# Router logits taken from unscaled residual rows, with the norm's gain folded into the router weights

## The chip, the cores and the metric

The kernel runs on one core of one Trainium2 chip. The metric is the device time of one execution in microseconds. TensorE (PE) multiplies and transposes, VectorE (DVE), ScalarE (ACT) and GpSimd (POOL) work on vectors, SyncE (SP) issues most of the transfers and POOL issues the indexed ones.

## What is computed

One inference step of two layers over 576 rows (512 prompt rows and 64 sample rows) of width 1024. Layer 0 mixes rows with a banded attention, layer 1 with a convolution module. Each mixer is followed by a mixture of experts: 4 groups of 8 experts, the best group, and in it the best two experts.

```python
xt  = rms_norm(x, norm_ffn)                     # x * rstd(row) * gain(column)
g   = softmax(xt @ w_group + b_group);          g_w, g_idx = top_k(g, 1)
e   = xt @ w_router + b_router                  # 32 logits, 8 of each group
v, i = top_k(e[group g_idx], 2);                w2 = softmax(v)
y   = sum over the two experts: g_w * w2 * (silu(xt @ w_gate) * (xt @ w_up)) @ w_down
x   = x + y
```

## The kernel before

All matrices are float32. The 576 rows are five tiles, numbers 0 to 4; tile 4, the last, has 64 rows. Each engine runs a fixed list of instructions and waits on counting semaphores; `steps.done` makes an engine wait for its own instruction. The order around the change is written out by hand.

**The projection stage** ends each mixer. TensorE runs `project_pe`: for each tile j two halves of 512 columns, eight matmuls each (L421); the last tile's halves are interleaved in `both_halves` (L435). Between them stand the router's small jobs for the tiles ahead: `turn_pe` transposes a tile (8 transposes, L346), `logits_pe` multiplies it with the 36 router columns (L954), `ranks_pe` (L966, L967) counts rows per expert, and `table_pe` (L977) builds a table of the rows that each expert takes.

**VectorE** runs `project_dve`: `add(j, h)` adds a projected half to the residual `x` and counts `proj_ev` (L466); in layer 1 a full-width bias is added first (L475). `norm_dve` takes the reciprocal of the row's root (L327, from ScalarE's square sum and root, L320 and L321) and writes `x * ss * gain` to `xf` (L332), counting `normed`. `turn_dve` copies the second half of the transposed tile out of PSUM (L358), ScalarE's `turn_act` the first. `choose_dve` picks group and experts in three parts (L997 to L1001, L1005 to L1010, L1012 to L1024), `slots_dve` (L1029 to L1036) and `table_dve` (L1046 to L1051) work out where the rows go. The last `table_dve` ends the stage and counts `tabled`.

**SyncE** runs `first_loads(l, 1)` through this stage, strictly in order. For tiles 0 to 3 it waits for `normed` and stores the tile of `xf` to `x_rows` in HBM (L1371). Then:

```python
sp.wait_ge(proj_mm, 2 * TILES * (l + 1))
gu_load(sp, l, 1, (0,))            # 2 MB
x_store(TILES - 1)                 # waits for normed of the last tile
gu_load(sp, l, 1, (1,))            # 2 MB
gu_load(sp, l, 2, (0,))            # 2 MB
gu_part(sp, l, 2, 1, ONE, 0, UNSHARED)   # 0.5 MB
```

In layer 1 one more load of 2 MB (`dn_load`, L1357) stands behind these.

**The experts.** GpSimd waits for `x_out` (all five stores landed) and `tabled`, and fetches the rows of the first two expert pairs from `x_rows` with indexed transfers (`rows_in`, L1112). TensorE bridges the time with `keep_running` (L1188; 12 matmuls, which stand in the trace as 24), transposes the rows of pair 0 (L1195), and runs 16 pairs: up and gate (L1205) and down (L1224). The weights of a later pair are issued as TensorE frees their place; for pair 3 this happens in three parts during the first pair's L1205.

Of the kernel before, what the change touches and what calls it, by code (L numbers as in the profile page):

```python
# [7 lines left out]
ALU = mybir.AluOpType  # L8
# [3 lines left out]
P = 128  # L12
# [32 lines left out]
def encoder(nc, x_prompt, x_sample, cache_attn_k, cache_attn_v, cache_conv,  # L45
# [10 lines left out]
    C = D // P  # L56
# [29 lines left out]
    with ExitStack() as ctx:  # L86
        def sb(name, shape, dt=F32):
            return ctx.enter_context(nc.sbuf_tensor(name, shape, dt))

        def sem(name):  # L90
            return ctx.enter_context(nc.semaphore(name))
# [22 lines left out]
        mean_w = sb("mean_w", [P, P])  # L114
        router_w = sb("router_w", [P, C, RC])
        router_b = sb("router_b", [P, RC])
        logits = sb("logits", [P, TILES, RC])
        ss = sb("ss", [P, 3, TILES])
        eps = sb("eps", [P, 1])
# [55 lines left out]


        xf = xt_flat[:].rearrange("p (j d) -> p j d", j=TILES)
        xf_pc = xt_flat[:].rearrange("p (j q c) -> p j c q", j=TILES, c=C)
        xw = work[:, 0:C * TOKENS].rearrange("p (c t) -> p c t", c=C)
        junk = work[:, C * TOKENS:C * TOKENS + D]  # L180
        EARLY_TILES = 4 * C * FE // D - TILES
# [91 lines left out]
        op_mm = sem("op_mm"); op_ev = sem("op_ev"); krow_mm = sem("krow_mm"); krow_ev = sem("krow_ev")  # L273
        kv_out = [sem(f"kv_out{s}") for s in range(2)]

        first_up = sem("first_up"); proj_mm = sem("proj_mm"); proj_ev = sem("proj_ev")

        route_mm = sem("route_mm"); gates_max = sem("gates_max"); gates_exp = sem("gates_exp"); picks = sem("picks"); ranks = sem("ranks"); summed = sem("summed")
        routed = sem("routed"); ranked = sem("ranked"); placed = sem("placed"); far_routed = sem("far_routed")
# [56 lines left out]

        def turn_pe(pe, n, j):
            r, at = rows[j], TILES * n + j
            pe.wait_ge(normed, at + 1)
            if at >= 2:  # L340
                pe.wait_ge(turn_ev_a, at - 1)
                pe.wait_ge(turn_ev_d, at - 1)
            src = xf_pc if n % 2 else xn_pc
            for c in range(C):
                b = bank[TURN_BANKS[at % 2][c // 4]]
                mm = nc.tensor.transpose(b[:, (c % 4) * P:(c % 4) * P + r], src[0:r, j, c, :],  # L346
                                         ident[0:r, 0:r])
            mm.then_inc(turned, 1)
# [17 lines left out]
        def norms_act(act, steps, n):  # L366


            for j in range(TILES + 1):
                if j >= 1 and n % 2:  # L370
                    turn_act(act, n, j - 1)
                if j < TILES:
                    norm_act(act, steps, n, j)
                if j >= 1 and n % 2 == 0 and n < 2 * LAYERS:
                    turn_act(act, n, j - 1)
# [82 lines left out]

        def project_dve(dve, steps, l, bias_row):
            LAST = TILES - 1  # L460

            def add(j, h):
                dve.wait_ge(proj_mm, 2 * TILES * l + 2 * j + h + 1)
                r, cols = rows[j], slice(h * HALF, (h + 1) * HALF)
                src = bank[3][h * DEC:(h + 1) * DEC, :] if j == LAST else bank[h if l == j == 0 else 3 + h][0:r, :]
                nc.vector.tensor_tensor(x[0:r, j, cols], x[0:r, j, cols], src, ALU.add).then_inc(proj_ev, 1)  # L466

            for j in range(TILES):
                if j == LAST:
                    turn_dve(dve, 2 * l + 1, j - 1)  # L470
                    table_dve(dve, steps, l, j - 3)
                    slots_dve(dve, steps, l, j - 2)
                if bias_row is not None:
                    r = rows[j]
                    steps.done(nc.vector.tensor_tensor(x[0:r, j, :], x[0:r, j, :], bias_row[0:r, :], ALU.add))  # L475
                add(j, 0)
                if j == LAST:
                    add(j, 1)
                    choose_dve(dve, steps, l, j - 1, 0)
                    norm_dve(dve, steps, 2 * l + 1, j)  # L480
                    choose_dve(dve, steps, l, j - 1, 1)
                    turn_dve(dve, 2 * l + 1, j)
                    choose_dve(dve, steps, l, j - 1, 2)
                    continue
                if j >= 1:
                    turn_dve(dve, 2 * l + 1, j - 1)
                    if j >= 3:
                        table_dve(dve, steps, l, j - 3)
                    for part in range(3):
                        choose_dve(dve, steps, l, j - 1, part)  # L490
                add(j, 1)
                norm_dve(dve, steps, 2 * l + 1, j)
                if j >= 2:
                    slots_dve(dve, steps, l, j - 2)
            choose_dve(dve, steps, l, LAST, 0)
            table_dve(dve, steps, l, LAST - 2)
            slots_dve(dve, steps, l, LAST - 1)
            choose_dve(dve, steps, l, LAST, 1)
            choose_dve(dve, steps, l, LAST, 2)
            table_dve(dve, steps, l, LAST - 1)  # L500
            slots_dve(dve, steps, l, LAST)
            table_dve(dve, steps, l, LAST)
# [432 lines left out]


        def logits_at(j):
            return bank[4 if j >= TILES - 2 else 5][0:rows[j], 0:RC]

        def logits_pe(pe, l, j):  # L940
            pe.wait_ge(turn_ev_a, TILES * (2 * l + 1) + j + 1)
            pe.wait_ge(turn_ev_d, TILES * (2 * l + 1) + j + 1)
            if j == 0:
                pe.wait_ge(small_in, 64 * (l + 1))
            if j == TILES - 1:
                pe.wait_ge(picks, TILES * l + j - 1)
            elif j == TILES - 2:
                pe.wait_ge(proj_ev, 2 * TILES * l + 2 * (j + 1))
            elif TILES * l + j >= 1:
                pe.wait_ge(picks, TILES * l + j)  # L950
                if j >= 2:
                    pe.wait_ge(tabled, TILES * l + j - 1)
            for c in range(C):
                mm = nc.tensor.matmul(logits_at(j), xw[:, c, j * P:j * P + rows[j]], router_w[:, c, :],  # L954
                                      start=c == 0, stop=c == C - 1)
            mm.then_inc(route_mm, 1)
# [31 lines left out]
        def choose_dve(dve, steps, l, j, part):  # L988
# [5 lines left out]
            few = down_iota[0:r, EXPERTS - GROUPS:EXPERTS]  # L994
            if part == 0:
                dve.wait_ge(route_mm, TILES * l + j + 1)
                do(V.tensor_tensor(logits[0:r, j, :], logits_at(j), router_b[0:r, :], ALU.add))  # L997
                do(V.tensor_reduce(t(0), lg, AX.X, ALU.max))
                do(V.scalar_tensor_tensor(some[:, 0:GROUPS], lg, t(0), few, ALU.is_equal, ALU.mult))
                do(V.tensor_reduce(t(1), some[:, 0:GROUPS], AX.X, ALU.max))  # L1000
                do(V.tensor_scalar(pen[0:r, :], few, t(1), -BIG, ALU.not_equal, ALU.mult))  # L1001
                return
# [765 lines left out]
        def _(sp):  # L1768
# [8 lines left out]
            for l in range(LAYERS):  # L1777
# [3 lines left out]
                sp.dma_start(gain[:, 0, :], broadcast(norm_ffn[l])).then_inc(gain_in, 16)  # L1781
                for src, dst in ((w_group[l], router_w[:, :, 0:GROUPS]), (w_router[l], router_w[:, :, GROUPS:RC])):
                    sp.dma_start(dst, src.rearrange("(p c) n -> p c n", c=C)).then_inc(small_in, 16)
                for src, dst in ((b_group[l], router_b[:, 0:GROUPS]), (b_router[l], router_b[:, GROUPS:RC])):
                    sp.dma_start(dst, broadcast(src)).then_inc(small_in, 16)
                if l == 1:
# [138 lines left out]
```

## Time and profile before

| | us |
|---|---|
| median of 3 runs | 1281.15 (1277.71 to 1281.42) |
| profiled execution, its own time | 1276.23 |
| its span | 1274.6 |
| PE / DVE / ACT / POOL busy in the span | 1072.0 / 493.7 / 289.5 / 272.3 |
| layer 0: projections begin, first expert rows land | 318.4, 404.6 |
| layer 1: projections begin, first expert rows land | 869.2, 974.1 |

The span runs from the first to the last instruction on the core; the execution's own time is 1.6 us more. The projection stage with its tail of router work takes about 86 us in layer 0 and 105 us in layer 1, the expert stages about 270 us each.

### The profile page before, as it was taken

To read this page: it belongs to the slowest core of one execution; us is meant where nothing else is said; L and a number is where in the kernel's file an instruction comes from. 1 tells how busy PE (TensorE), PEld (TensorE's weight loads), DVE (VectorE), ACT (ScalarE), POOL (GpSimd) and SP (SyncE) were. 2 spreads that over 40 slices of the span, in tenths; PEclk is the share of its full clock that TensorE was granted. 3 is DMA by queue.
4 is the path that set the end of the run, shared out by engine and by line. 5 is a ranking of instruction groups with operands and counts; after the bars stand their busy time and mean duration, and the time that the engine had idled before them with its cause. 6 is when DMAs were issued, how large, how long until landed. Compare 5 with 4: busy or idle time off the path is not lost.

```text
span 1274.6 us, 14578 instructions
## 1 busy us (share of the span) xinstructions
PE 1072.0 (84%) x5326; PEld 621.2 (49%) x5326; DVE 493.7 (39%) x1066; ACT 289.5 (23%) x616; POOL 272.3 (21%) x289
## 2 busy tenths in 40 slices
PE   6999999998996978777746999987986978787780
PEld 5777777774545333333315777653544333333320
DVE  3234444344356211111115799984554111111116
ACT  3233232333111101000003455553111101000002
POOL 3000000001003211001051488850003111100033
PEclk9999999999997989888887999998996989998895
DMA  8953322302707999999955912000037999999963
GB/s 279 389 174 110 109 96 78 105 25 106 297 34 280 412 420 419 421 421 421 391 165 141 374 37 71 25 25 12 32 108 290 396 421 421 421 420 421 378 258 131
DMA packets 110287, 303.68 MB, mean 238 GB/s; under 512 B 18440, under 2 KB 65672, under 8 KB 86521
## 3 DMA queue, kind: packets, MB, share of 16 engines
q1 hardware_dynamic: 87977, 254.74, 51.8%
q0 software_dynamic: 22256, 48.22, 10.4%
q8 instruction: 33, 0.54, 0.2%
q14 instruction: 21, 0.17, 0.0%
HBM read 278.34 MB, written 57.12 MB: 263 GB/s over the span
## 4 chain that ended last, share of the span: by engine, by line
PE 58%; DMA 21%; DVE 10%; issue 8%; ACT 2%; SPq 1%; POOL 0%; DVEq 0%; POOLq 0%
PE bank L1205 12%; PE bank L522 10%; DMA ring<-in_w_up 8%; DMA arena<-in_w_up 8%; PE bank L421 7%; PE bank L1224 6%; PE bank L549 4%; DVE bank L1711 2%; PE bank L1507 2%; PE bank L572 2%; PE bank L1195 2%; PE bank L588 2%; PE bank L613 2%; PE bank L346 1%; DMA work<-in_w_pw 1%
## 5 line engine op out<-in xcount | busy, mean ns | idle before, releaser
L1205 PE MATMUL bank<-ring,work 128*64 128x512 f32 x704 | 170.1, 639 | 30.4 <-DMA ring<-in_w_up 28.6
L1224 PE MATMUL bank<-ring,work 128*64 128x512 f32 x528 | 125.5, 619 | 36.2 <-DVE work L1243 23.8
L1507 PE MATMUL bank<-arena,work 128*128 128x288 f32 x512 | 129.6, 416 | 8.0 <-issue 3.6
L522 PE MATMUL bank<-arena,ring 128*128 128x288 f32 x512 | 131.9, 412 | 0.4 <-issue 0.4
L1205 PEld LDWEIGHTS bank<-ring,work 128*64 128x64 f32 x704 | 58.4, 147 | 139.3 <-issue 136.9
L1239 DVE TENSOR_TENSOR work<-work,bank 128x256 f32<-128x256 f32 x33 | 13.9, 420 | 287.9 <-ACT work L1235 287.9
L1507 PEld LDWEIGHTS bank<-arena,work 128*128 128x128 f32 x512 | 99.2, 195 | 37.9 <-issue 8.0
L1658 POOL TENSOR_TENSOR ring<-ring 128x606 f32<-128x606 f32 x76 | 103.6, 1363 | 55.3 <-ACT ring L1607 45.7
L522 PEld LDWEIGHTS bank<-arena,ring 128*128 128x128 f32 x512 | 94.9, 190 | 33.0 <-issue 8.4
L421 PE MATMUL bank<-ring,arena 128*128 128x512 f32 x224 | 101.2, 605 | 6.6 <-ACT arena L1642 6.6
L1205 PE MATMUL bank<-arena,work 128*64 128x512 f32 x352 | 86.2, 646 | 19.7 <-DMA arena<-in_w_up 18.7
L1711 DVE SCALAR_TENSOR_TENSOR bank<-work,ring,bank 128x606 f32<-128x606 f32 x129 | 98.8, 844 | 0.0
L1224 PEld LDWEIGHTS bank<-ring,work 128*64 128x64 f32 x528 | 36.9, 141 | 102.0 <-issue 73.2
L1112 POOL DMA_INDIRECT work<-x_rows,tok_at x32 | 33.0, 1030 | 214.3 <-DVEq L1051 205.1
L1235 ACT ACTIVATE work<-bank 128x256 f32<-128x256 f32 x33 | 12.7, 384 | 276.7 <-PE bank L1205 276.7
L1607 ACT ACTIVATE ring<-work,ring 128x606 f32<-128x606 f32 x84 | 65.4, 797 | 36.9 <-POOL ring L1658 36.9
L421 PEld LDWEIGHTS bank<-ring,arena 128*128 128x128 f32 x224 | 42.3, 194 | 55.6 <-issue 53.8
L1205 PEld LDWEIGHTS bank<-arena,work 128*64 128x64 f32 x352 | 29.3, 149 | 75.2 <-issue 75.2
L1116 POOL DMA_INDIRECT y_sorted<-work,slot_at x16 | 15.8, 986 | 228.0 <-DVE work L1251 228.0
L728 ACT ACTIVATE work<-work,soft 64x192 f32<-64x192 f32 (+4 forms) x80 | 42.6, 533 | 85.8 <-DVE soft L814 85.8
L916 POOL DMA_DIRECT2D out<-work x8 | 4.6, 573 | 249.3 <-ACT work L721 249.3
L549 PEld LDWEIGHTS bank<-ring,arena 128*128 128x128 f32 x448 | 51.1, 192 | 5.3 <-issue 5.3
(258 smaller groups left out, 1297.7 us busy)
## 6 DMA issues: line engine op xcount, KB each, us to landing
ring<-in_w_down SPq DMA_DIRECT2D x32, 2048.0 KB, 24.5
ring<-in_w_gate SPq DMA_DIRECT2D x20, 2048.0 KB, 21.6
ring<-in_w_up SPq DMA_DIRECT2D x20, 2048.0 KB, 30.7
arena<-in_w_gate SPq DMA_DIRECT2D x10, 2048.0 KB, 22.5
arena<-in_w_up SPq DMA_DIRECT2D x8, 2048.0 KB, 32.8
ring<-in_w_qkv SPq DMA_DIRECT2D x24, 512.0 KB, 6.1
y_sorted<-gain POOLq DMA_DIRECT2D x8, 1536.0 KB, 5.7
work<-in_w_pw SPq DMA_DIRECT2D x16, 512.0 KB, 5.2
```

The source lines that it names most:

```text
L421: mm = nc.tensor.matmul(bank[3 + h][0:rows[j], :], act_t[:, c, j * P:j * P + rows[j]], w[:, c, h * HALF:(h + 1) * HALF], start=c == 0, sto ...
L522: mm = nc.tensor.matmul(bank[b][:, 0:HT], wa[s][:, w, c, :], xt[:, c, h * HT:(h + 1) * HT], start=c == 0, stop=c == C - 1)
L549: mm = nc.tensor.matmul(bank[0][:, j * P:(j + 1) * P], xt_tile(c, j), wa[s][:, 2, c, :], start=c == 0, stop=c == C - 1)
L572: mm = nc.tensor.matmul(bank[3 + h][:, 0:nk], qt[s][hd, q0:q0 + P], kt[s][hd, k0:k0 + nk], start=True, stop=True)
L728: ins = nc.scalar.activation(prob[0:q, b, h, 0:nk], prob[0:q, b, h, 0:nk], ACT.Exp, bias=soft[0:q, b, 0, h:h + 1], accum_out=soft[0:q, b, ...
L1112: pool.indirect_dma_start(xe[local % 2], None, x_rows, bass.IndirectOffsetOnAxis(tok_at[:, local:local + 1], 0), bounds_check=TOKENS - 1, ...
L1205: mm = nc.tensor.matmul(bank[2 + s][rr, :], xte[s][:, c, rr], wgu[g][:, :, e, c, :], start=c == 0, stop=c == C - 1)
L1224: mm = nc.tensor.matmul(bank[5 + h][rr, :], hts[:, c, rr], wdn[s][:, e, c, h * HALF:(h + 1) * HALF], start=c == 0, stop=c == FC - 1)
L1507: mm = nc.tensor.matmul(bank[banks[h][w]][:, 0:GT], wp[s][:, w, c, :], xt[:, c, h * GT:(h + 1) * GT], start=c == 0, stop=c == C - 1)
L1607: nc.scalar.activation(out, u[s][:, m:m + OUTS], ACT.Copy, scale=cvec[s][:, m:m + 1]).then_inc(prod_done, 1)
L1658: pool.tensor_tensor(side[s], side[s], prod[turn(s, m)], ALU.add).then_inc(side_done, 1)
L1711: steps.behind(V.scalar_tensor_tensor(a, src(t), w(t), a, ALU.mult, ALU.add))
```

## The change

The transposes read the residual `x` itself once its two halves are added, instead of the scaled rows `xf`. The column gain of the norm goes into the router weights: it is loaded a second time, one value per partition and chunk (`gain_pc`, a small DMA issued by SyncE in both layers), and VectorE multiplies `router_w` with it once a layer at the start of `project_dve`. The row factor is applied when the bias is added to the logits. The scaled rows are still written to `xf`, since the experts take them.

For the last tile, `norm_dve` stands behind all three parts of the choice for tile 3. Both halves of the transposed tiles 3 and 4 are copied by ScalarE. The last tile's logits go to PSUM bank 3. In layer 1 the bias of tile j+1 is added behind the norm of tile j, ahead of `slots_dve`, where it stood ahead of tile j+1's first add.

```diff
@@ turn_pe
-            pe.wait_ge(normed, at + 1)
+            if n % 2:
+                pe.wait_ge(proj_ev, 2 * TILES * (n // 2) + 2 * (j + 1))
+            else:
+                pe.wait_ge(normed, at + 1)
...
-            src = xf_pc if n % 2 else xn_pc
+            src = x_pc if n % 2 else xn_pc
@@ norms_act
                     turn_act(act, n, j - 1)
+                    if j >= TILES - 1:
+                        turn_copy(act, nc.scalar.copy, n, j - 1, 1, turn_ev_d)
@@ project_dve
+            dve.wait_ge(small_in, 80 * (l + 1))
+            nc.vector.tensor_tensor(router_w[:], router_w[:], gain_pc[:].unsqueeze(2).to_broadcast([P, C, RC]),
+                                    ALU.mult).then_inc(router_scaled, 1)
...
-            for j in range(TILES):
-                if j == LAST:
-                    turn_dve(dve, 2 * l + 1, j - 1)
-                    table_dve(dve, steps, l, j - 3)
-                    slots_dve(dve, steps, l, j - 2)
+            def add_bias(j):
                 if bias_row is not None:
                     r = rows[j]
                     steps.done(nc.vector.tensor_tensor(x[0:r, j, :], x[0:r, j, :], bias_row[0:r, :], ALU.add))
+
+            for j in range(TILES):
+                if j == LAST:
+                    table_dve(dve, steps, l, j - 3)
+                    slots_dve(dve, steps, l, j - 2)
+                if j == 0:
+                    add_bias(0)
                 add(j, 0)
                 if j == LAST:
                     add(j, 1)
                     choose_dve(dve, steps, l, j - 1, 0)
+                    choose_dve(dve, steps, l, j - 1, 1)
+                    choose_dve(dve, steps, l, j - 1, 2)
                     norm_dve(dve, steps, 2 * l + 1, j)
-                    choose_dve(dve, steps, l, j - 1, 1)
-                    turn_dve(dve, 2 * l + 1, j)
-                    choose_dve(dve, steps, l, j - 1, 2)
                     continue
...
                 norm_dve(dve, steps, 2 * l + 1, j)
+                add_bias(j + 1)
                 if j >= 2:
                     slots_dve(dve, steps, l, j - 2)
@@ logits_at, logits_pe
-            return bank[4 if j >= TILES - 2 else 5][0:rows[j], 0:RC]
+            b = {TILES - 1: 3, TILES - 2: 4}.get(j, 5)
+            return bank[b][0:rows[j], 0:RC]
...
-                pe.wait_ge(small_in, 64 * (l + 1))
+                pe.wait_ge(router_scaled, l + 1)
@@ choose_dve
-                do(V.tensor_tensor(logits[0:r, j, :], logits_at(j), router_b[0:r, :], ALU.add))
+                do(V.scalar_tensor_tensor(logits[0:r, j, :], logits_at(j), ss[0:r, 2, j:j + 1], router_b[0:r, :], ALU.mult,
+                                          ALU.add))
@@ sync block
+                sp.dma_start(gain_pc[:], norm_ffn[l].rearrange("(p c) -> p c", c=C)).then_inc(small_in, 16)
```

## Rows read from the trace of the kernel before

**Rows 1.** Page of the profile, part 4: shares of the chain that ended last.

```profile
PE 58%; DMA 21%; DVE 10%; issue 8%; ACT 2%; SPq 1%; POOL 0%; DVEq 0%; POOLq 0%
```

**Rows 2.** Chain that ended last, in order: start us, us, what.

```profile
400.29 4.26 DMA work<-x_rows,tok_at
...
406.65 7.09 PE bank L1205 x32
...
608.08 33.42 DMA ring<-in_w_up
...
713.09 16.57 DMA work<-in_w_pw
...
965.86 8.21 DMA work<-x_rows,tok_at
```

**Rows 3.** Timeline of VectorE, layer 0: start us, us, instruction, [idle before it].

```profile
319.58 0.69 DVE L466 TENSOR_TENSOR x<-x,bank 128x512 f32<-128x512 f32 x1 [1.24 <-PE bank L413]
...
382.01 1.39 DVE L466 TENSOR_TENSOR x<-x,bank 64x512 f32<-64x512 f32 x2
383.52 0.20 DVE L997 TENSOR_TENSOR logits<-bank,router_b 128x36 f32<-128x36 f32 x1
...
385.03 0.15 DVE L327 RECIPROCAL ss<-ss 64x1 f32<-64x1 f32 x1 [0.40 <-ACT ss L321]
385.22 1.27 DVE L332 SCALAR_TENSOR_TENSOR arena<-x,ss,gain 64x1024 f32<-64x1024 f32 x1
...
387.80 0.42 DVE L358 COPY work<-bank 128x256 f32<-128x256 f32 x1 [0.20 <-PE bank L346]
...
390.25 0.19 DVE L997 TENSOR_TENSOR logits<-bank,router_b 64x36 f32<-64x36 f32 x1 [0.54 <-PE bank L954]
```

**Rows 4.** Timeline of TensorE at the tails of layer 0 and layer 1.

```profile
381.51 1.98 PE L954 MATMUL bank<-router_w,work 128*128 128x36 f32 x16
...
388.33 1.89 PE L954 MATMUL bank<-router_w,work 128*64 128x36 f32 x16 [0.63 <-ACT work L358]
...
398.31 4.86 PE L1188 MATMUL bank<-ident 128*128 128x128 f32 x24
404.59 1.16 PE L1195 MATMUL bank<-ident,work 128*128 128x128 f32 x8 [1.42 <-DMA work<-x_rows,tok_at]
...
974.11 1.97 PE L1195 MATMUL bank<-ident,work 128*128 128x128 f32 x8 [4.80 <-DMA work<-x_rows,tok_at]
976.99 9.86 PE L1205 MATMUL bank<-ring,work 128*64 128x512 f32 x32 [0.90 <-ACT work L1230]
```

**Rows 5.** Timeline of SyncE's DMA issues: start us, us, transfer.

```profile
386.52 0.52 SPq L1371 DMA_DIRECT2D x_rows<-arena  x1
...
694.67 1.60 SPq L1785 DMA_DIRECT2D router_b<-in_b_group  x1
...
952.24 0.54 SPq L1371 DMA_DIRECT2D x_rows<-arena  x1
952.82 0.59 SPq L1344 DMA_DIRECT2D ring<-in_w_up  x1
```

**Rows 6.** Timeline of VectorE, layer 1: the last bias and the last choice.

```profile
946.49 1.21 DVE L475 TENSOR_TENSOR x<-x,ring 64x1024 f32<-64x1024 f32 x1
...
955.97 0.19 DVE L997 TENSOR_TENSOR logits<-bank,router_b 64x36 f32<-64x36 f32 x1 [0.54 <-PE bank L954]
```

**Rows 7.** DMA queues (packets, MB, share) in 398:400, 402:402.3, 968:970, 970:970.5 us.

```profile
q1 hardware_dynamic: 135, 0.84, 99.6%
...
q0 software_dynamic: 10, 0.04, 85.5%
...
q1 hardware_dynamic: 99, 0.81, 97.9%
...
q0 software_dynamic: 12, 0.05, 23.9%
```

**Rows 8.** Busy by window (us, engines, granted clock, DMA) around both gathers.

```profile
402.20:402.40 0.20, 0.20 (x3) 0.20 (x3) 0.20 (x1) 0.00 (x0) 0.20 (x1) 0.61 1.21 184
...
972.40:972.60 0.20, 0.00 (x0) 0.00 (x0) 0.00 (x0) 0.00 (x0) 0.20 (x1) 0.50 0.87 308
```

More of the change, by code:

```diff
@@ L116, in encoder @@
         router_b = sb("router_b", [P, RC])
+        gain_pc = sb("gain_pc", [P, C])
         logits = sb("logits", [P, TILES, RC])
@@ L177, in encoder @@
         xf = xt_flat[:].rearrange("p (j d) -> p j d", j=TILES)
-        xf_pc = xt_flat[:].rearrange("p (j q c) -> p j c q", j=TILES, c=C)
+        x_pc = x[:].rearrange("p j (q c) -> p j c q", c=C)
         xw = work[:, 0:C * TOKENS].rearrange("p (c t) -> p c t", c=C)
@@ L274, in encoder @@
         kv_out = [sem(f"kv_out{s}") for s in range(2)]
-        first_up = sem("first_up"); proj_mm = sem("proj_mm"); proj_ev = sem("proj_ev")
+        first_up = sem("first_up"); router_scaled = sem("router_scaled"); proj_mm = sem("proj_mm"); proj_ev = sem("proj_ev")
         route_mm = sem("route_mm"); gates_max = sem("gates_max"); gates_exp = sem("gates_exp"); picks = sem("picks"); ranks = sem("ranks"); summed = sem("summed")
```

## The prediction

> **What bounds the kernel now.** I read the page's chain first [rows 1]: TensorE carries 58% of it, transfers 21%. The chain in order of time says where [rows 2]: in both expert stages weight loads are waited for (one of 33.42 us stands here for several), so an expert stage is a stream of weights whose end moves with its start. The stream starts when the first pair's matmuls free the places of pair 0 in parts, and those matmuls wait for `x_rows` to be fetched by index. So the question for this change is one of two instants: when do the first expert rows land, 404.55 us in layer 0 (400.29 plus 4.26) and 974.07 in layer 1 (965.86 plus 8.21)?
>
> The two fetches differ. Layer 0's takes 4.26 us, layer 1's 8.21. The DMA queues show why [rows 7]: SyncE's queue (q1) has 99.6% of the engines at 398 to 400 us and then falls off, and the first packets of GpSimd's queue (q0) are seen at 402, 1.7 us after the issue. In layer 1, q1 still has 97.9% at 968 to 970, and q0's first packets are seen at 970.0, 4.1 us after the issue. The fetch stands behind SyncE's prefetched weights. These were issued behind the store of the last tile's scaled rows, at 386.52 and 952.24 [rows 5], and that store waits for `normed` of tile 4. The change moves that instant.
>
> **The tail of VectorE, layer 0.** VectorE runs without a real pause from 382 us to the end of the stage. Now [rows 3]: the adds of tile 4 end at 383.4, part 0 of the choice for tile 3 starts at 383.52, the norm of tile 4 stands inside the choice (L332 at 385.22), a copy of 0.42 follows at 387.80, and the choice for tile 4 starts at 390.25. After: the copy of tile 3 has gone to ScalarE, so the adds begin as soon as TensorE turns from the projection to L954 at 381.51 [rows 4], and end at 382.9. The choice cannot use that: its logits leave TensorE at 383.49 (381.51 and 1.98), as before. From there to 390.25 are 6.73 us; out of them go the copy (it holds up the next instruction by 0.34) and three idle times, 0.40 ahead of L327, 0.20 ahead of the copy and 0.54 ahead of L997. That leaves 5.25 us: the choice for tile 4 starts at 388.77, **1.45 us earlier**. TensorE keeps up: it can transpose tile 4 at 383.6 (1.2 us), ScalarE copies both halves by 385.6 (two copies of 0.4), and the 1.89 us of L954 [rows 4] end at 387.6, against 388.3 plus 1.9 now. From there to `tabled` nothing else changes: the stage's end and the issue of the fetch come 1.45 us earlier, 398.85.
>
> But the norm of tile 4 is now the last thing ahead of that choice: its L332 starts at about 387.5 and ends at 388.85, where it ended at 386.5. **The last store and all that SyncE issues behind it come 2.35 us later**: up of pair 1, gate and part of up of pair 2, in layer 1 also a down matrix. SyncE stands waiting; nothing on its queue can pass.
>
> **Layer 1.** The bias of tile 4 (1.21 us, L475 [rows 6]) went ahead of tile 4's adds, behind `slots`. It now stands ahead of `slots(1)`, for whose `placed` TensorE waits in the middle of the last projection, so TensorE ends that projection 1.2 us later, at about 947.2. The adds lose nothing (they were held by the bias itself): they end at 948.5 and the logits of tile 3 come at 949.2. Plus the same 5.25 us gives 954.5 for the choice of tile 4, against 955.97 [rows 6], again 1.45 earlier; the norm ends at 954.6 against 952.2, again 2.4 later.
>
> **What becomes of the fetch.** In layer 1 the fetch already has to wait for the stream. Its issue moves 1.45 us earlier, to 964.4, and the stream ends 2.4 later: it lands **2.4 us later**, 976.5. In layer 0 the stream gave way at about 400.3, and now does at 402.65, where the fetch is 3.8 us old. From q0's first packets to the landing were 2.55 us in layer 0 (402.0 to 404.55) and 4.1 in layer 1 (970.0 to 974.07): it lands at 405.2 to 406.75. I take 405.75, **1.2 us later**. The bounds of this term are 1.45 us earlier (issue alone counts) and 2.35 later (the whole shift of the stream).
>
> The chip's two kinds of queues could share instead. The Trainium skill, DMA: Bandwidth & Descriptors, section Queues, rings and completion order, says that each DMA engine takes turns between the queues it has work for, packet by packet. By that the fetch would not stand behind the stream, and this term would be 1.45 us of gain in each layer. The trace disagrees as far as it goes: q0 got nothing until 970.0.
>
> **The clock.** TensorE's idle time ahead of the first transposes decides it. In layer 0 the 24 bridging matmuls end at 403.17, the rows land after an idle time of 1.42 us [rows 4], and the clock has just risen to full (0.61 in the mean of 402.2 to 402.4 [rows 8]) and stays. In layer 1 the idle time is 4.80 us, and the granted clock is 0.50, the 1.2 GHz level, at 972.4, ahead of the rows. The price is in the first pair: L1205 takes 9.86 us there and 7.09 in layer 0, L1195 1.97 and 1.16, together 3.6 us. After the change layer 0's bridge ends 1.45 us earlier, at 401.7, and the rows land at 405.75: 4.0 us idle. That is far nearer to the 4.80 that lost the clock than to the 1.42 that kept it, so layer 0 pays too: **3.6 us**, bounds 0 and 4.3. Layer 1 has lost it already; its idle time grows without a further price that I can read.
>
> **The small parts.** `gain_pc` is one more issue in SyncE's list. In layer 0 that list is long done. In layer 1 it stands just ahead of the router biases (694.67 [rows 5]), the second projection matrix and the weights of pair 0, behind which the convolution's next weights wait, and for these the chain waits 16.57 us [rows 2]. SyncE's issues cost 0.52 to 1.60 us [rows 5]; one that isn't spread to all partitions by a broadcast, as the one of 1.60 is, is nearer to the first: **0.5 us**, bounds 0 and 1.6. The multiplication of `router_w` (288 columns) costs less than the 0.69 us of a 512-column add, and VectorE idles 1.24 us ahead of the first projected half [rows 3]; in layer 1 it waits for the first projection in the same way: nothing. Were that cover gone it would cost 0.5. The first operation of part 0 gets a multiplication: 0.03 us, five times a layer, nothing. In tiles 0 to 3 the earlier transposes gain nothing, since TensorE is never seen to wait for `normed` between the projections; its order is fixed.
>
> **The sum.** Layer 0: 1.2 for the fetch and 3.6 for the clock; layer 1: 2.4 for the fetch and 0.5 for the issue. Together 7.7 us. The profiled execution took 1276.23 us (span 1274.6 and 1.6 around it), so its like would take 1283.9; against the median of 1281.15, 4.9 us above the profiled one, the forecast is **1288.9 us**, 0.6% slower.
>
> **Rivals.**
>
> A, the clock holds in layer 0: all else as above, 4.1 us, 1285.3. For it speaks that the fetch might land at 405.2, or sooner; against it that even then the idle time is 3.5 us.
>
> B, the fetch takes its share of the engines at once (the rule of the skill named above). Then the stage's end decides: 1.45 us gained twice, 0.5 lost for the issue, the clock in layer 0 kept since its idle time stays at 1.4: 2.4 us faster, 1278.8, which is not slower. It decides as soon as q0's packets begin within 2 us of the issue while q1 is full. Against it stands layer 1's 4.1 us.
>
> C, the streams of weights are not moved by their start: the stages would absorb up to 7 us and the time stays within 1 us of before, 1281 to 1282. Against it: the stream runs at one level through both stages, with such waits in it. Were there slack at its end, these waits would not be on the chain.
>
> D, a larger loss: layer 0 pays the whole 2.35, the clock 4.3, the issue 1.6, and layer 1 stays at the low clock longer by 1 us: 11.7 us with the 2.4 of layer 1, 1292.8.
>
> **How the numbers follow.** This kernel's three runs lie 0.3% apart, so a change under 0.3% (3.8 us) tells nothing. The forecast has 0.5, A 0.23, B 0.12, C 0.08, D 0.05; 0.02 is left for a gain over 0.3% by something I do not see. Slower by over 0.3%: the forecast, D and half of A (its 4.1 us lies at the bound), 0.66. Within: half of A, B, C, 0.32. Faster: 0.02. The range runs from 1280.5, between B and C, to 1292: outside lie B, most of D and half of the left case, 0.17.
>
> **What would show it.** Right, if in the changed profile the choice for tile 4 starts about 5.3 us after the one for tile 3, the last store of each layer comes 2.4 us later and ahead of nothing else on SyncE, the fetch of layer 1 takes about 12 us (8.21 plus 1.45 plus 2.4) and that of layer 0 about 7, TensorE idles about 4 us ahead of L1195 in layer 0, and the first L1205 there takes nearly 10 us. Wrong, if q0's packets come in while q1 is full, if the clock is full at layer 0's first pair, or if the later start of the stream is not found again at its end.

## The result, and the profile after

Over 18 timed runs of each kernel the changed one took 1284.29 us in the median (1282.24 to 1289.66), the one before 1281.5 (1277.71 to 1284.23). The ratio is **1.0027** with a 95% interval of 1.0017 to 1.0037: 3.5 us slower (0.0027 of 1281.5), between 2.2 and 4.7. That is a loss, against the 7.7 us forecast, and it lies just under the bound of 0.3%. Two slow executions among the twelve of the run before_again, of 2202 and 2755 us, are left out of its figures below. The profiled execution took 1284.28 us (span 1282.6), 8.05 more than that of before.

The page of the profile after, part 4, the shares of the chain that ended last, against [rows 1]:

```profile
PE 57%; DMA 21%; DVE 10%; issue 8%; ACT 2%; POOL 1%; SPq 1%; DVEq 0%; POOLq 0%
```

The shares say nothing. The chain in order of time does, against [rows 2]; L1209 and L1219 are what L1195 and L1205 were:

```profile
387.55 1.28 DVE arena L333
...
398.84 6.72 DMA work<-x_rows,tok_at
405.60 1.58 PE bank L1209 x8
...
408.07 9.52 PE bank L1219 x32
...
592.34 36.96 DMA arena<-in_w_up
...
717.20 17.38 DMA work<-in_w_pw
...
972.98 9.54 DMA work<-x_rows,tok_at
982.57 1.97 PE bank L1209 x8
...
985.44 9.26 PE bank L1219 x32
```

The last tile's norm (L333) stands on the chain as it did before (L332 at 385.22 us), 2.3 us later; the first fetch of layer 0 takes 6.72 us instead of 4.26, and its first pair's matmuls 9.52 instead of 7.09. Layer 1's fetch takes 9.54 instead of 8.21, not the 12 that I expected.

VectorE in layer 0, the timeline that answers to [rows 3] (start us, us, instruction, idle before it):

```profile
381.52 1.40 DVE L475 TENSOR_TENSOR x<-x,bank 64x512 f32<-64x512 f32 x2 [2.06 <-PE bank L441]
383.43 0.26 DVE L1010 SCALAR_TENSOR_TENSOR logits<-bank,ss,router_b 128x36 f32<-128x36 f32 x1 [0.51 <-PE bank L967]
...
387.55 1.28 DVE L333 SCALAR_TENSOR_TENSOR arena<-x,ss,gain 64x1024 f32<-64x1024 f32 x1
388.75 0.24 DVE L1010 SCALAR_TENSOR_TENSOR logits<-bank,ss,router_b 64x36 f32<-64x36 f32 x1
```

SyncE's last stores, against [rows 5]:

```profile
388.85 0.52 SPq L1385 DMA_DIRECT2D x_rows<-arena  x1
...
963.13 0.53 SPq L1385 DMA_DIRECT2D x_rows<-arena  x1
```

TensorE at both tails, against [rows 4]:

```profile
405.60 1.57 PE L1209 MATMUL bank<-ident,work 128*128 128x128 f32 x8 [3.25 <-DMA work<-x_rows,tok_at]
408.07 9.52 PE L1219 MATMUL bank<-ring,work 128*64 128x512 f32 x32 [0.91 <-ACT work L1244]
...
948.48 0.38 PE L979 MATMUL bank<-before,ones 128*128 128x32 f32 x2 [2.43 <-DVEq L1046]
...
949.06 1.98 PE L441 MATMUL bank<-ring,arena 128*64 128x512 f32 x4
...
951.21 1.60 PE L441 MATMUL bank<-ring,arena 128*64 128x512 f32 x4
...
982.57 1.97 PE L1209 MATMUL bank<-ident,work 128*128 128x128 f32 x8 [6.07 <-DMA work<-x_rows,tok_at]
```

In layer 0 the instants are those of the forecast: the choice for tile 4 starts at 388.75 (forecast 388.77), the store is issued at 388.85, the fetch at 398.84 (398.85), its rows land at 405.56 (405.75). TensorE idles 3.25 us (4.0). In layer 1 something stands that I had not seen: an idle time of 2.43 us in the middle of the last projection, with matmuls of 1.98 and 1.60 us behind it. The busy times by window of the same profile show the granted clock (the number ahead of the last two) there and at layer 0's first pair:

```profile
407.00:409.00 2.00, 1.09 (x5) 0.37 (x6) 1.47 (x6) 1.78 (x2) 1.59 (x2) 0.50 0.06 1
...
946.00:948.00 2.00, 0.06 (x2) 0.00 (x0) 1.96 (x3) 0.00 (x0) 0.00 (x0) 1.00 0.28 113
948.00:950.00 2.00, 1.52 (x8) 0.87 (x10) 0.98 (x5) 0.00 (x0) 0.00 (x0) 0.73 0.37 150
950.00:952.00 2.00, 2.00 (x14) 0.87 (x12) 0.39 (x2) 0.00 (x0) 0.00 (x0) 0.50 0.04 8
```

VectorE in layer 1 tells what TensorE waits for: the bias of tile 4 (L480), and behind it the slots of tile 1, whose copy (L1045) releases L979:

```profile
946.55 1.21 DVE L480 TENSOR_TENSOR x<-x,ring 64x1024 f32<-64x1024 f32 x1
947.80 0.25 DVE L1043 TENSOR_SCALAR qcmp_flat<-hot,token_no 128x64 f32<-128x64 f32 x1
948.09 0.19 DVE L1045 COPY rank_sb<-bank 128x32 f32<-128x32 f32 x1
```

### The profile page after: what moved, and what is told of

It reads as the page before. It is cut to its first block, busy times and chain, and to the rows that moved or that the text cites. A ratio compares the mean times of both kernels' runs of the same rounds, so it can differ in the third digit from the quotient of the medians.

```text
span 1282.6 us, 14577 instructions
## 1 busy us (share of the span) xinstructions
PE 1081.8 (84%) x5326; PEld 623.5 (49%) x5326; DVE 493.4 (38%) x1064; ACT 291.0 (23%) x620; POOL 272.2 (21%) x289
## 4 chain that ended last, share of the span: by engine, by line
PE 57%; DMA 21%; DVE 10%; issue 8%; ACT 2%; POOL 1%; SPq 1%; DVEq 0%; POOLq 0%
DMA arena<-in_w_up 16%; PE bank L1219 12%; PE bank L534 10%; PE bank L427 7%; PE bank L1238 6%; PE bank L561 4%; PE bank L1521 2%; DVE bank L1725 2%; PE bank L584 2%; PE bank L1209 2%; PE bank L600 2%; PE bank L625 2%; PE bank L350 1%; DMA work<-in_w_pw 1%; DMA work<-x_rows,tok_at 1%
## 5 line engine op out<-in xcount | busy, mean ns | idle before, releaser
L1219 PE MATMUL bank<-ring,work 128*64 128x512 f32 x704 | 174.8, 654 | 30.7 <-DMA ring<-in_w_up 28.9
L1238 PE MATMUL bank<-ring,work 128*64 128x512 f32 x528 | 124.5, 615 | 34.0 <-DVE work L1257 22.5
L1219 PEld LDWEIGHTS bank<-ring,work 128*64 128x64 f32 x704 | 58.8, 150 | 144.4 <-issue 143.1
L1219 PE MATMUL bank<-arena,work 128*64 128x512 f32 x352 | 88.3, 659 | 17.6 <-DMA arena<-in_w_up 15.7
L1219 PEld LDWEIGHTS bank<-arena,work 128*64 128x64 f32 x352 | 29.8, 151 | 74.7 <-issue 74.7
```

What stands on the lines that cost most here:

```text
L1219: mm = nc.tensor.matmul(bank[2 + s][rr, :], xte[s][:, c, rr], wgu[g][:, :, e, c, :], start=c == 0, stop=c == C - 1)
L1238: mm = nc.tensor.matmul(bank[5 + h][rr, :], hts[:, c, rr], wdn[s][:, e, c, h * HALF:(h + 1) * HALF], start=c == 0, stop=c == FC - 1)
```

## The experiments

Stages in us, each from instants of a profile: "tail" is from the first projected half's add (in layer 1 from the projection's first matmul) to the transposes of the first expert rows, "experts" from there to VectorE's first sum of expert rows into `x`, "mixer 1" the convolution between.

| profile | tail 0 | experts 0 | mixer 1 | tail 1 | experts 1 |
|---|---|---|---|---|---|
| before | 85.0 | 261.3 | 203.3 | 104.9 | 276.8 |
| the same kernel, 3 further | 84.8 to 85.2 | 262.0 to 266.2 | 203.5 to 205.4 | 104.8 to 105.5 | 275.8 to 278.0 |
| after, both profiles | 85.9 | 263.8 | 206.1 | 107.1 | 276.5, 274.3 |
| norm_early | 84.0 | 263.7 | 205.2 | 106.7 | 277.1 |
| bias_back | 86.0 | 265.1 | 205.0 | 104.4 | 275.9 |
| both_back | 83.4 | 262.7 | 205.7 | 103.4 | 274.7 |
| after_hold | 83.5 | 264.5 | 206.2 | 101.8 | 280.6 |
| both_hold | 83.5 | 264.3 | 205.6 | 98.6 | 282.3 |

The tails repeat to within 0.8 us where a kernel was profiled more than once; the expert stages scatter by up to 5.

**The unchanged kernels again.** Each was timed again beside the variants.

> The kernel before, unchanged, profiled a second time. The profiled execution of before took 1276.23 us and the median of its runs is 1281.5; the profiled one of after took 1284.28 at a median of 1284.29. Theory: the profiled execution of before was a fast one of its kind, because TensorE's clock held across layer 0's idle time of 1.4 us ahead of the first expert transposes; a second profile then shows the clock lost there in layer 0 (first up and gate matmuls near 9.9 us instead of 7.09) and a span near 1279 to 1280. Rival: the clock is full there again, the profile lies near 1276, and the missing 5 us stand somewhere else. Time ratio to before 1.000.

> The changed kernel, unchanged, profiled a second time. Theory (the shift in the single stages is that of the two profiles, the whole of 8 us is not: one of before's timed runs in three is 2 to 3 us above the next): layer 0's fetch again lands between 405.5 and 406.5 us, 6.7 us after its issue, the idle time ahead of the first expert transposes is over 3 us with the clock lost, and layer 1's tail is again near 107 us against 104.8. The span lies 1 to 4 us from 1282.6, median 1284 to 1285. Rival: the lost clock or the stall in layer 1's last projection is missing in this profile, and was chance.

Here and below stand the median, the ratio to before and its 95% interval. Before: 1281.15 us, 1.0003 [0.999, 1.0016]; in its profile (span 1276.8) the clock fell within the first pair of layer 0, whose L1205 took 8.68 us, where 9.9 were expected. After: 1284.76, 1.0039 [1.0025, 1.0054]; its profile repeats the idle times of 3.20 us ahead of L1209 and 2.43 in layer 1's projection. The loss is real; the two ratios give 3.5 and 5.0 us.

**The norm of tile 4 back inside the choice for tile 3**, all else as after:

```diff
                     choose_dve(dve, steps, l, j - 1, 0)
+                    norm_dve(dve, steps, 2 * l + 1, j)
                     choose_dve(dve, steps, l, j - 1, 1)
                     choose_dve(dve, steps, l, j - 1, 2)
-                    norm_dve(dve, steps, 2 * l + 1, j)
```

> The changed kernel with the norm of tile 4 put back between part 0 and part 1 of the choice for tile 3; the choice for tile 4 starts when it did. Theory (the late store is the cost): the last store is issued 2.8 us earlier, at about 386.1 us in layer 0, the fetch there lands at 403 to 404 instead of 405.6, the idle time ahead of the transposes falls from 3.25 to 1.0 to 1.7 us and the clock holds; layer 1's fetch lands 1 to 2.5 us earlier. Median 3 to 6 us below the changed kernel, 1279 to 1281. Rival (the place of the norm doesn't matter, the fetch has a latency of its own under load): the fetch takes the same time from its issue, and the time stays within 1 us of the changed kernel's 1284.3.

1281.15 us, 0.9996 [0.998, 1.0012]. The store of layer 0 is back at 386.69 us (after: 388.85), TensorE's idle time ahead of the transposes falls from 3.25 to 2.47, tail 0 is 1.9 shorter, tail 1 only 0.4. The clock was expected to hold in layer 0 and does not: L1219 takes 8.80 us. By the ratios (1.0027 less 0.9996) the late norm costs about 4 us; the tails show 2.3 of them, nearly all in layer 0.

**The bias back ahead of its own tile's adds**, all else as after:

```diff
-                if j == 0:
-                    add_bias(0)
+                add_bias(j)
                 add(j, 0)
...
                 norm_dve(dve, steps, 2 * l + 1, j)
-                add_bias(j + 1)
```

> The changed kernel with the projection bias of tile j added directly ahead of tile j's first add again (for tile 4 behind the slots of tile 2). Theory: in layer 1 TensorE's idle time ahead of the rank matmuls in the last projection falls from 2.43 us to 1.2, the clock is not lost there, and the bias of tile 4 fits in VectorE's 2.6 us of idle time ahead of the last adds: layer 1's tail is 2.5 to 3 us shorter, median 1281.5 to 1282. Rival: the fetch of layer 1 is held by the weight stream, which moves only with the store, so it lands as late as the stream allows; a gain of 1 us or less.

1280.96 us, 1.0002 [0.9988, 1.0016]. Tail 1 is 2.7 shorter than after and 0.4 shorter than before, though the store is still late there. TensorE's idle time in the last projection is 1.18 us. Its timeline in this kernel, layer 1's last projection:

```profile
948.46 1.08 PE L441 MATMUL bank<-ring,arena 128*64 128x512 f32 x4
949.57 1.06 PE L441 MATMUL bank<-ring,arena 128*64 128x512 f32 x4
```

The same groups took 1.98 and 1.60 in after. So the loss of tail 1 hangs on the bias: a stall of 2.43 us, and a clock that falls behind it. The same place in before, which is not among the rows ahead, with the same three groups:

```profile
940.38 0.38 PE L966 MATMUL bank<-before,ones 128*128 128x32 f32 x2 [1.12 <-DVEq L1032]
...
940.91 1.08 PE L435 MATMUL bank<-ring,arena 128*64 128x512 f32 x4
...
942.02 1.06 PE L435 MATMUL bank<-ring,arena 128*64 128x512 f32 x4
```

The idle time is 1.12 us there, and the matmuls are as fast as bias_back's. By the ratios (1.0027 less 1.0002) the early bias costs 3.2 us, of which tail 1 shows 2.7.

**Both moves undone.** What is left of the change is the folded gain, the transposes of `x` and ScalarE's copies. It was timed twice.

> The changed kernel with both moves undone: norm of tile 4 between part 0 and part 1 of the choice for tile 3, and the bias directly ahead of its tile's first add. Each alone brought 3 us against the changed kernel (1281.15 and 280.96 against 1284.3; read 1280.96). Theory (two separate costs, the late store in both layers, the stall and the low clock in layer 1's last projection): they add up, median 1277.5 to 1279, ratio to before 0.997 to 0.9985, and both tails are shorter than before's. Rival (both act on one thing, the landing of layer 1's fetch behind the weight stream): 1280 to 1281, no better than either.

> The kernel with both moves undone again, now beside the version with both gain columns loaded early. It had a ratio of 0.9958 to before on one chip, the other version 0.9975 on another. Theory (the extra load's place costs over 1 us): this one is at least 1 us slower than the other here. Rival (the place costs 0.35 us or nothing): within 1 us. Ratio to before 0.995 to 0.998 in either case.

1276.06 us, **0.9958** [0.9943, 0.9973], and 1275.76, **0.9959** [0.9943, 0.9974]: faster than before by 5.4 and 5.3 us by the ratios, and than after_again, timed beside it, by 8.7. The two moves alone gave back 4.0 and 3.2 us; together they give no less than their sum. The tails are shorter than before's by 1.6 and 1.5 us. In layer 0 that is the 1.45 that I had computed for an earlier choice of tile 4. In layer 1 the choice and the fetch's issue come 2.4 us earlier, counted from the projection's start: in before the adds of tile 4 stood behind the copy of tile 3 and the bias and ended at 949.13 us, 1.2 us after the logits of tile 3 were ready (947.95), and that delay is gone as well. From the issue to the transposes it then takes 1.0 us longer. And beside bias_back, whose only difference is the late norm, tail 0 is 2.6 and tail 1 is 1.0 shorter: that is what the late store costs in each, besides what single profiles scatter. The chain of this kernel in layer 1:

```profile
965.93 8.86 DMA work<-x_rows,tok_at
```

The fetch is issued at the instant of before [rows 2], although the three stages ahead took 2.1 us longer in this profile (551.8 against 549.7).

**More bridging matmuls**, 24 instead of 12, in after, in both_back and in before:

```diff
-            keep_running(12)
+            keep_running(24)
```

> The changed kernel with 24 bridging matmuls ahead of each expert stage instead of 12 (48 in the trace). Theory (the lost clock costs about 3 us in each layer): TensorE stays busy until the rows land, the first up and gate matmuls take 7.1 us in both layers instead of 9.5 and 9.3, and the median falls by 4 to 6 us to about 1279. Rival (the low clock is hidden behind the weight stream): the first matmuls are faster, but the time stays within 1 us of 1284.3. If the bridge is longer than the fetch, up to 1 us of the gain is lost in each layer.

> The kernel with both moves undone and 24 bridging matmuls ahead of each expert stage. With 24 in the changed kernel the first up and gate matmuls in layer 0 took 7.09 us instead of 9.52, but idle times that the profile puts down to issue came earlier and gave back half, and the median fell by 1.2 us. Theory: the same here, 0.5 to 1.5 us below the kernel with both moves undone. Rival: with the fetch of layer 0 landing at 404, the idle time there is too short to lose the clock in most executions, and the longer bridge ends after the rows have landed: 0 to 1 us slower than with 12.

> The kernel before with 24 bridging matmuls ahead of each expert stage instead of 12. In its first profile the clock held in layer 0 and the first up and gate matmuls took 7.09 us; in its second, with 1.15 us idle ahead of the transposes, the clock fell in the first pair and they took 8.68. Theory (most executions of before pay this already): with the longer bridge they take 7.1 in layer 0, and layer 1, 4.8 us idle, has its clock back in part; 0.5 to 2 us faster than before. Rival (it mostly held): the bridge only delays the transposes, 0.5 us or more slower.

1283.11 us, 1.0015 [1.0004, 1.0026]; 1276.54, 0.9963 [0.9946, 0.9979]; 1279.54, 0.9987 [0.9972, 1.0001]. In after the bridge does what it should, TensorE's timeline:

```profile
405.72 1.16 PE L1209 MATMUL bank<-ident,work 128*128 128x128 f32 x8 [0.64 <-issue]
407.79 7.09 PE L1219 MATMUL bank<-ring,work 128*64 128x512 f32 x32 [0.91 <-ACT work L1244]
```

The clock is kept and 2.43 us of L1219 come back, but the median gains only 1.2 us (1.5 by the ratio to after's first timing, 3.1 to its second). That speaks against a price of 3.6 us, without excluding it. Two things stand against each other in keep24's profile: from the first transposes to the second pair's matmuls it takes 14.84 us, where after took 17.69, and its tail 1 is 0.9 us longer than after's, since the low clock behind the stall in the last projection lasts longer there (L441 1.98 and 1.95 us). With both moves undone, the longer bridge gains nothing; in before it reads 1.7 us of gain, between 0 and 3.6.

**Two more profiles of before**, for the clock's price.

> The kernel before, a third profile. Theory (its first profile was a lucky execution, in most the clock falls inside layer 0's first pair although TensorE idles only 0.8 to 1.5 us ahead of it): first up and gate matmuls near 8.7 us. Rival (the clock mostly holds): 7.09 us.

> The kernel before, a fourth profile, with the same two expectations: near 8.7 us for the first up and gate matmuls of layer 0 if the clock mostly falls there, 7.09 if it mostly holds.

1282.44 and 1284.25 us. In both the clock is full in layer 0's first pair (7.09 us), as in [rows 4], and both nevertheless reach the second pair nearly as late as after does. From the first transposes to the second pair's matmuls are 14.84 us in the first profile, 17.33 and 17.11 in these two, 16.89 in before_again with its low clock, 17.69 and 17.63 in after and after_again. ScalarE and TensorE in before_p4:

```profile
408.91 1.28 ACT L1235 ACT_TABLE_LOAD   x1
416.25 0.38 ACT L1235 ACTIVATE work<-bank 128x256 f32<-128x256 f32 x1 [6.06 <-remote]
...
417.22 0.50 PE L1214 MATMUL bank<-ident,work 128*128 128x128 f32 x2 [2.37 <-DVE work L1239]
```

The up and gate matmuls end at 413.8 us, but the first `silu` (L1235) starts only at 416.25, 7.3 us behind the start of its table load, and what it waits for isn't recorded ("remote"). TensorE then stands 2.37 us for its product. In the profile on which I built the forecast that stretch was 4.6 us (409.17 to 413.78). In after:

```profile
410.31 1.28 ACT L1249 ACT_TABLE_LOAD   x1
417.63 0.38 ACT L1249 ACTIVATE work<-bank 128x256 f32<-128x256 f32 x1 [6.04 <-PE bank L1219]
```

There it is 7.3 as well, but the matmuls end only at 417.6 us and are its last release. In keep24, at full clock, ScalarE waits for nothing else either:

```profile
415.06 0.39 ACT L1249 ACTIVATE work<-bank 128x256 f32<-128x256 f32 x1 [3.76 <-PE bank L1219]
```

The 18 profiles of all variants give the whole picture of this stretch, from the first transposes to the second pair's matmuls in layer 0. Eight have L1205 or L1219 at full clock (7.09 us). In five of them the first `silu` comes 6.5 to 7.4 us behind its table load and the stretch takes 17.1 to 18.5 us; in three (before, keep24, both_keep24) it comes after 4.6 to 5.0, and the stretch takes 14.8 to 15.4. Ten have the low clock in that group (8.6 to 9.5 us), and the stretch takes 16.9 to 18.1. The means are 16.6 and 17.5 us. So the low clock costs up to 2.9 us in an execution without ScalarE's wait, next to nothing in one with it, and some 0.8 us in the mean.

**The extra load alone, and loaded early.** Before with `gain_pc`'s transfer and the wait for it but no use of it, and both_back with both layers' columns loaded in layer 0:

```diff
                     sp.dma_start(dst, src.rearrange("(p c) n -> p c n", c=C)).then_inc(small_in, 16)
+                sp.dma_start(gain_pc[:], norm_ffn[l].rearrange("(p c) -> p c", c=C)).then_inc(small_in, 16)
```

```diff
-                sp.dma_start(gain_pc[:], norm_ffn[l].rearrange("(p c) -> p c", c=C)).then_inc(small_in, 16)
+                if l == 0:
+                    for n in range(LAYERS):
+                        sp.dma_start(gain_pc[:, n, :], norm_ffn[n].rearrange("(p c) -> p c", c=C)).then_inc(small_in, 16)
```

> The kernel before with nothing but the extra load of the gain (one value per partition and chunk) in SyncE's list and the wait for it. Theory of the prediction: its issue costs 0.5 us in layer 1 ahead of the convolution's weights and is passed on; median 0.3 to 0.7 us above before. Rival: the convolution's weights wait for the DMA engines and not for the issue, or the load's small pieces hold them: 0, or over 1 us. The convolution stage took 203.3 and 203.5 us in two profiles of before and 206.1 in the changed kernel's.

> The kernel with both moves undone, and both layers' gain columns loaded in layer 0's list, where SyncE has time, so that layer 1's list is as in the kernel before. Ahead of before alone the extra load cost 1.6 us (interval 0 to 3.7), and the convolution stage took 205.0 to 206.1 us in seven of eight profiles with it, and 203.3 and 203.5 in two without. Theory (the load costs over 1 us in layer 1): the convolution stage falls to 203.5, median 1274 to 1275.3. Rival (its issue of 0.35 us is all it costs, the rest is scatter): 1275.7 or more.

> Both moves undone and both gain columns loaded early, on the same chip as the version without the early load. Theory: median 1 us or more below it. Rival: within 1 us of it.

The load alone: 1281.61 us, 1.0015 [1.0000, 1.0029]. Early: 1277.28, 0.9975 [0.9958, 0.9993], and 1277.47, 0.9971 [0.9958, 0.9985], the second time, beside both_back's 0.9959. Taking the issue out of layer 1's list gained nothing in time; its 0.5 us can't be told from zero here. The profiles lean the other way: mixer 1 takes 202.8 and 203.7 us in the two with the early load, 203.6 to 206.4 (205.6 in the mean) in the eleven with the load in layer 1's list, and 203.3 to 205.4 in the five without it. A cost of 1 us or more in that stage isn't excluded.

**SyncE holds back its prefetch.** SyncE waits for the first fetched rows before it issues the loads of pair 2:

```diff
                 gu_load(sp, l, 1, (1,))
+                sp.wait_ge(base.x_in[1], 16 * (EPAIRS // 2 * l + 1))
                 gu_load(sp, l, 2, (0,))
```

> The changed kernel with SyncE waiting for the first fetched rows before it prefetches the weights of pair 2 (and, in layer 1, the down matrix of pair 1). This takes 2.6 MB in layer 0 and 4.7 MB in layer 1 out of the stream ahead of the fetch. Theory of the prediction (the fetch stands behind SyncE's stream): it lands 4.3 us after its issue in both layers, where the changed kernel took 6.7 and 9.6 us, the clock holds better in layer 0, and the tails are 2.4 and 5.3 us shorter. The weights held back use DMA time that was idle until the first pair's parts are issued, so most of it stays: median 1278 to 1281 against 1284.3. Rival: the fetch's time is its own latency under any load, 6.5 us or more; or the tails shorten, but the weights that come later are missed at pair 2, and the time is 1284 or more.

> The same wait in the kernel with both moves undone (median 1276.06, ratio 0.9958). There the fetch took 4.3 us from its issue in layer 0 and 9.2 in layer 1. Theory: only layer 1 gains, up to 4.9 us in its tail, of which the prefetch of 4.7 MB gives back a part: median 1272 to 1275. Rival: no gain, since the weight stream as a whole starts as late as before: 1276 or more.

1284.2 us, 1.0022 [1.0007, 1.0037], and 1280.12, 0.9988 [0.9972, 1.0004]. The chain of the former:

```profile
399.37 4.29 DMA work<-x_rows,tok_at
403.71 1.17 PE bank L1209 x8
...
409.54 5.79 another core or an unknown queue
```

The fetch takes 4.3 us in layer 0 instead of 6.7 and 4.2 in layer 1 instead of 9.5; the tails are 2.4 and 5.3 us shorter. And the time is that of after, because the expert stage of layer 1 is 4 to 6 us longer than in after. Part of it is that the weights held back are missed later: TensorE's waits for up matrices in that stage come to 24.9 us instead of 21.5, and in both_hold to 25.2 instead of 21.8. The rest isn't resolved. In both_hold the hold costs 4 us. The chain's wait of 5.79 us here is ScalarE's, ahead of the first `silu`, again at full clock.

The queues show how the fetch and the stream meet (packets, MB, share of the engines). After, 977.5 to 978 us, 4.5 us behind the issue:

```profile
q1 hardware_dynamic: 40, 0.17, 85.9%
q0 software_dynamic: 8, 0.03, 16.9%
```

And the first half microsecond of the fetch in after_hold, layer 1, 973.5 us, with nothing on q1:

```profile
q0 software_dynamic: 18, 0.07, 104.8%
```

With q1 empty the first packets come 1.6 us behind the issue in both layers. With q1 full they come 4.0 to 4.5 behind it in layer 1, in before [rows 7], after, bias_back and both_back, whether the store was early or late; then both queues run side by side. So in layer 1 the delay goes with the issue, not with the stream's end.

## Why the prediction was wrong

The direction was right, and the time lies in its range. What failed in size is the clock's term (step 3), and what failed in its reasons is the path in layer 1 (step 4). Step by step:

1. **The tail of VectorE, layer 0**: right to 0.02 us, the choice at 388.75, the store 2.3 us later.

2. **What becomes of the fetch, layer 0** (1.2 us): tail 0 is 0.9 longer. Right. norm_early and both_back show the cause: with the store early again and the gain of 1.45 us kept, tail 0 is 1.9 and 2.5 us shorter than after.

3. **The clock** (3.6 us in layer 0): **this step failed, by its size.** The clock was lost as foreseen, after 3.25 us of idle time instead of 4.0, and L1219 took 2.4 us longer. But they end beside a wait of ScalarE that in most executions holds the first pair anyway: it stands in both further profiles of before that kept the clock. From the first transposes to the second pair's matmuls after takes 17.6 to 17.7 us, before 17.1 and 17.3 in the two further profiles that keep the clock: 0.3 to 0.6 us instead of 3.6, and 0.8 in the mean over all 18 profiles. The whole loss says the same: of its 3.5 to 5.0 us the tails show 0.9 and 2.2 (steps 2 and 4), which leaves 0.4 to 1.9 for the clock and the issue together, where the sum had 4.1. I had set the low clock's price against one of the few executions in which nothing hid it; in such a one it is 2.9 us, as keep24's profile shows. Why ScalarE starts so late in the others stays open: no run took the table load or its neighbours apart.

4. **What becomes of the fetch, layer 1** (2.4 us): the size came out by luck, tail 1 is 2.2 longer, but **the cause was wrong**. The issue was to come 1.45 us earlier and the fetch to take 12. From the projection's start the issue comes 0.9 us later (97.5 against 96.6), and the fetch takes 9.5, 1.3 more than before. That the fetch lands when the stream ends is false: q0 gets its share about 4 us behind its issue. The trace of before had shown it, in the view that [rows 7] takes q0's first packets from (970 to 970.5 us), where the stream still has most of the engines:

```profile
q1 hardware_dynamic: 19, 0.16, 73.4%
```

bias_back has the same late store and a tail 1 that is 0.4 us shorter than before: its fetch is issued 2.0 us earlier and takes 1.5 longer. I did see that the bias stands ahead of `slots(1)` and ends the projection later, and wrote that "the adds lose nothing". They lose: TensorE's idle time ahead of L979 grew from 1.12 to 2.43 us, the clock fell to 0.50 behind it, the 1.2 GHz level, and eight projection matmuls and the small ones between them ran 1.6 us longer (1.98, 0.56 and 1.60 against 1.08, 0.36 and 1.06). This is the mechanism of step 3, at a place where I had not looked for it.

5. **The issue** (0.5 us): not to be resolved in time. The load alone reads 1.9 us, [0, 3.7], and removing it from layer 1 gave nothing. In after's profile SyncE's list from `gain` to the projection's matrix takes 4.7 us, 0.6 more than before's 4.1 (before_again: 4.5). The reason given was wrong, though: `gain_pc`'s issue takes 2.03 us and the broadcast behind it 0.43, so the 1.60 us of [rows 5] belonged to the place in the list and not to the broadcast.

6. **The execution read.** The profiled execution of before, 1276.23 us, lies under all 18 timed runs of that kernel, and its span of 1274.6 under those of four further profiles (of it or of it with the spare load), 1276.8 to 1282.6. The forecast stood on the median of 1281.15, within 0.4 us of the one measured beside after, so its base is not where it went wrong; the price of the clock is, read from that one execution. The sum of 7.7 comes close to the difference of the two profiles, 8.05, and that too is luck: 2.5 of these are the expert stage of layer 0 and 2.8 the convolution, and between profiles of the kernel before these stages scatter by 4.8 and 2.0.

Of the rivals, A (no price for the clock, 4.1 us) came nearest in size, 1285.3, though the clock did fall. B was wrong for the delay and half right for what comes after it. The Trainium skill (DMA: Bandwidth & Descriptors, section Queues, rings and completion order) says that the engines take turns between queues. The trace of layer 1 agrees once q0 has packets (16.9% for it beside q1's 85.9%); the 4 us ahead of them the rule does not explain. C was wrong in saying that the start of an expert stage doesn't matter: both_back gains by it. But it holds for a start that is bought by holding weights back.

What the rest of the change is worth shows in both_back: a gain of 5.3 to 5.4 us, of which the tails show 3.1. Between the choices for tiles 3 and 4 VectorE's list is rid of the copy and the idle times of [rows 3], with the norm early as well as late. Where the other 2 us arise the profiles don't tell, since the long stages scatter by more; nor were the folded gain and ScalarE's copies run apart. The two moves that came with it cost 4.0 and 3.2 us.

## What to carry to other kernels

A saving on one engine's list and a reordering beside it should be timed apart: here the first gained 5 us, the second lost 9. Before you move an instruction ahead of another, list every engine that waits behind it, and where TensorE is one of them count its idle time and then the clock. And take the price of a disturbance from several profiles of the same kernel: in one of them it can stand bare, while in most something else hides it.

## What the runs showed of the hardware

- An idle time of 2.43 us in the middle of a dense projection lowered the granted clock to 0.50 for the following matmuls (four in 1.98 us instead of 1.08) in all five profiles with the early bias (after, after_again, norm_early, keep24, after_hold); the same place in before (1.12 us) and in bias_back and both_back (1.18) did not.
- A GpSimd fetch by index has its first packets 1.6 us behind the issue when SyncE's queue is empty, and 4.0 to 4.5 us when it is full (3.8 in layer 0 of after); in layer 1 it takes 4.2 us in all in the one case and 8.2 to 9.8 in the other. A full queue delays it by 2.4 to 2.9 us and then shares with it.
- ScalarE's first `silu` of layer 0 began 7.1 to 7.4 us behind the start of its table load in before_p3, before_p4 and after_hold, though its input had been ready for about 2.5 us; in the first profile of before it was 4.6 us, in keep24 5.0 and in both_keep24 4.9, at the same full clock. What holds it isn't recorded.
- Four profiles of the unchanged kernel spread over 8 us of 1280 in their spans (1274.6 to 1282.6), while its medians over five sets of 17 to 35 runs, on several chips, lay within 1.5 us (1279.98 to 1281.5).
